# A two-layer model on one core: the phases after the recurrence as one program with one weight stream

## The chip, the cores and the metric

The kernel runs on one core of one Trainium2 chip. Its engines are named as the profile names them: PE is TensorE (matmul), PEld its weight loads, DVE is VectorE, ACT is ScalarE, POOL is GpSimd, SP is SyncE, which here only issues DMAs. The metric is device time in microseconds of one execution. Lower is better.

## The reference, cut to what matters

The input is one sequence of 512 tokens with 1024 channels (`x`). Two blocks follow each other, all in float32:

```python
h = rms_norm(x, a_norm);  x = x + rwkv7_time_mix(h, ...)        # recurrence, then y @ a_w_out   (2048 -> 1024)
h = rms_norm(x, b_norm);  c, b, u, g = split(h @ b_w_in, 4)     # 1024 -> 4 * 2048
y = b * conv3(c * u) * silu(g);  x = x + y @ b_w_out            # 2048 -> 1024
x = rms_norm(x, final_norm)                                     # end of the first model
h = rmsnorm(x, norm1_g);  proj = h @ w_in                       # 1024 -> 2560, start of the second
mixed = [rg_lru(...) * gelu(...), stick_breaking(...), diff_attention(...)]
x = x + mixed @ w_out                                           # 1024 -> 1024
h2 = rmsnorm(x, norm2_g);  gate, val = split(conv3(h2 @ w_ff_up) + b, 2)   # 1024 -> 2 * 2816
x = x + (silu(gate) * val) @ w_ff_down                          # 2816 -> 1024
return rmsnorm(x, final_g)
```

`rms_norm(x, g)` is `x * rsqrt(mean(x*x over channels) + 1e-6) * g`: for each token one number (the norm factor) times the channel's gain.

## The kernel before

Activations lie with channels on the 128 partitions and the 512 tokens along the row; a "chunk" is 128 channels of all tokens, so `x` has DC = 8 chunks, the inner width IC = 16, the feed-forward width FC = 22. Every large product is made of three float32r matmuls of 128x128 weights on 128x512 data, from numbers split in a high and a low part: high weights by high data, high weights by low data, low weights by high data (L141, L142, L143 in `products`). The high part of a tile is an ACT copy, the low part a DVE subtraction (`split_lo`, L148), for the weights and for the activations.

The program is a row of phases, each a block of its own with its own buffers and semaphores. At the end of a phase all engines meet in a barrier and its semaphores are cleared (`Sems.clear`), so that no engine, and no DMA, works on the next phase before all are done with this one. Up to 900 us run `lerp_phase` and `rwkv_phase` (norm, mixing, the recurrence), which end with the tensor `gate`, the recurrence's output. Behind them, in this order:

- `out1` (`project_phase`): splits `gate` in `y`, multiplies by `w_out1` and adds to `x`; 8 output chunks `n` of two weight units each, where a unit is 8 of the 128x128 tiles (512 KB) and 24 matmuls. It sums the squares of the new `x` (ACT square, DVE add, one matmul with `row_mean`, L1367).
- `conv` (`conv_phase`): `head_scalar`, `head_vector` and `head_tensor` first make the norm factor (ACT: `Ln`, then `Exp`, each with a table load), scale `x` by gain and factor on DVE, and split it in `h`; then 16 chunks of 4 units, with gates and a convolution of 3 taps on DVE and ACT.
- `out2`, then the norm between the models on `x` (`norm_vector`, L177) and the variance for the next norm.
- `in2` (`input_phase`): head as before, 20 units, of which 16 leave channels on partitions (`proj`) and 4 have the data as the stationary operand and leave tokens on partitions (`vals`); the gated linear recurrence (`lru`) is worked off beside them on ACT, DVE and POOL, and PE makes its gates (L1686).
- `mixer_phase`: both attentions, four heads one after the other.
- `out3`, `up` (`up_phase`, 22 chunks of 2 units, head as before), `down` (22 chunks deep, two units of 11 tiles for each output chunk), and the last norm with the store.

Weight loads are issued by SP into two raw buffers of a phase (four in `in2`) and wait until DVE has split what lay there. Most chunks of `conv`, `up` and the projections run in hardware loops (`Fori`). Where the buffers lie in a partition of SBUF is fixed by their sizes and their order. The program built from the kernel has them at these byte addresses:

```
                      start   start mod 64
h_hi, h_lo            43264, 59648     0    data of conv, in2, up
y_hi, y_lo            163808, 131040   32   data of out1, out2
m_hi, m_lo            212960, 196576   32   data of out3
ff_hi, ff_lo          184288, 139232   32   data of down
out1/conv/out2/up w   84224, 100608    0    weights, high and low
out3 w                96512, 104704    0
in2 w                 122144, 138528   32
down w                54528, 77056     0
```

## Time and profile before

| | |
|---|---|
| median of 3 runs | 2247.37 us (2241.43 to 2247.61) |
| profiled execution, its own time | 2243.56 us |
| its span, first to last instruction | 2241.8 us |
| share of the span with PE / DVE / ACT / POOL busy | 89% / 54% / 41% / 4% |
| mean granted TensorE clock | 0.946 |
| moved by DMA | 154.18 MB, mean 69 GB/s |

The span is read from the profiler's trace of one execution, 1.76 us shorter than that execution's own time. A busy PE means that some matmul is in flight: a 128x512 matmul is shown with about 0.39 us, while the next one starts 0.23 us after it, so starts, not durations, give the pace.

### The profile page before, as it was taken

How to read it: one execution, taken by the hardware profiler on the slowest of the kernel's cores; microseconds unless marked ns; L12 is line 12 of the kernel's file. 1: busy time of each engine (PE TensorE's matmuls, PEld its weight loads, DVE VectorE, ACT ScalarE, POOL GpSimd, SP SyncE). 2: the span in 40 equal slices, each digit the busy share in tenths (PEclk: the TensorE clock that was granted, in tenths of full speed). 3: DMA queues.
4: the chain of work that ended last, by engine and by line, in shares of the span. 5: the costliest groups of instructions: out<-in, count | busy, mean ns of one | idle time of the engine just before them, and what ended most of it. 6: DMA issues, size and time to landing. Idle time of an engine off the chain costs nothing. (4 is left out here: it accounts for less than half of the span.)

```text
span 2241.8 us, 45147 instructions
## 1 busy us (share of the span) xinstructions
PE 2004.5 (89%) x19062; PEld 1541.2 (69%) x19062; DVE 1204.2 (54%) x1913; ACT 918.2 (41%) x1412; POOL 95.3 (4%) x122
## 2 busy tenths in 40 slices
PE   5989799999999997889999998969966689999797
PEld 3678567676666665667888886857843368888686
DVE  5562367777777775425434443354346446666332
ACT  3342355554646454323323322245345435555321
POOL 2000000000000000000000000001112000000000
PEclk8999899999999998899999999989977789999899
DMA  3225211111111100413233232232000022222321
GB/s 113 73 83 148 89 38 40 29 43 37 38 41 38 42 18 2 150 56 113 94 94 102 85 94 81 69 113 93 1 0 1 24 89 94 94 94 94 103 81 60
DMA packets 49269, 154.18 MB, mean 69 GB/s; under 512 B 8272, under 2 KB 10576, under 8 KB 48592
## 3 DMA queue, kind: packets, MB, share of 16 engines
q1 hardware_dynamic: 48960, 149.65, 20.8%
q8 instruction: 132, 2.16, 0.4%
q10 hardware_dynamic: 144, 2.10, 0.3%
q14 instruction: 33, 0.27, 0.0%
HBM read 145.43 MB, written 6.29 MB: 68 GB/s over the span
## 5 line engine op out<-in xcount | busy, mean ns | idle before, releaser
L141 PE MATMUL bank<-h_hi,conv_whi 128*128 128x512 f32 x512 | 200.6, 392 | 9.0 <-DVE h_lo L148 9.0
L142 PE MATMUL bank<-h_lo,conv_whi 128*128 128x512 f32 x512 | 200.3, 391 | 0.0
L143 PE MATMUL bank<-h_hi,conv_wlo 128*128 128x512 f32 x512 | 200.2, 391 | 0.0
L141 PE MATMUL bank<-h_hi,up_whi 128*128 128x512 f32 x352 | 138.5, 393 | 9.9 <-DVE h_lo L148 9.0
L1424 DVE TENSOR_TENSOR x<-x,bank 128x512 f32<-128x512 f32 x32 | 22.0, 687 | 220.7 <-PE bank L143 220.7
L142 PE MATMUL bank<-h_lo,up_whi 128*128 128x512 f32 x352 | 138.1, 392 | 0.0
L143 PE MATMUL bank<-h_hi,up_wlo 128*128 128x512 f32 x352 | 138.0, 392 | 0.0
L141 PE MATMUL bank<-xg_hi,g_hi 128*128 128x512 f32 x256 | 104.1, 406 | 25.0 <-DVE xg_lo L148 16.9
L141 PE MATMUL bank<-y_hi,out_whi 128*128 128x512 f32 x256 | 103.1, 403 | 22.5 <-DVE y_lo L148 12.9
L141 PEld LDWEIGHTS bank<-h_hi,conv_whi 128*128 128x128 f32 x512 | 96.8, 189 | 29.8 <-DVE h_lo L148 9.8
L143 PEld LDWEIGHTS bank<-h_hi,conv_wlo 128*128 128x128 f32 x512 | 96.8, 189 | 20.3
L142 PEld LDWEIGHTS bank<-h_lo,conv_whi 128*128 128x128 f32 x512 | 96.8, 189 | 20.2
L763 ACT ACTIVATE swapT<-invT 64x256 f32<-64x256 f32 x160 | 66.4, 415 | 106.0 <-DVE invT L1221 57.4
L142 PE MATMUL bank<-y_lo,out_whi 128*128 128x512 f32 x256 | 102.7, 401 | 0.0
L143 PE MATMUL bank<-y_hi,out_wlo 128*128 128x512 f32 x256 | 102.5, 400 | 0.0
L142 PE MATMUL bank<-xg_lo,g_hi 128*128 128x512 f32 x256 | 101.8, 398 | 0.0
L143 PE MATMUL bank<-xg_hi,g_lo 128*128 128x512 f32 x256 | 101.8, 398 | 0.0
L1377 ACT ACTIVATE out_whi<-out_raw 128x1024 fp32r<-128x1024 f32 (+1 forms) x48 | 44.0, 917 | 134.2 <-DMA out_raw<-in_w_out 68.5
L1511 ACT ACTIVATE conv_whi<-conv_raw 128x1024 fp32r<-128x1024 f32 x64 | 67.6, 1056 | 58.1 <-PE bank L143 51.8
L1199 DVE TENSOR_TENSOR low<-bank,con 128x512 f32<-128x512 f32 x80 | 55.1, 689 | 60.2 <-PE bank L904 60.2
L148 DVE TENSOR_TENSOR g_lo<-g_raw,g_hi 128x1024 fp32r<-128x1024 f32 x32 | 40.8, 1276 | 86.5 <-ACT g_hi L383 86.5
L904 PEld LDWEIGHTS bank<-inv,LA 64*64 64x64 f32 x2560 | 47.0, 135 | 58.2 <-issue 58.0
(362 smaller groups left out, 4984.5 us busy)
## 6 DMA issues: line engine op xcount, KB each, us to landing
conv_raw<-in_w_conv SPq DMA_DIRECT2D x64, 512.0 KB, 3.5
up_raw<-in_w_up SPq DMA_DIRECT2D x44, 512.0 KB, 3.7
out_raw<-in_w_out SPq DMA_DIRECT2D x32, 512.0 KB, 4.0
down_raw<-in_w_down SPq DMA_DIRECT2D x16, 704.0 KB, 4.5
in_raw<-in_w_in SPq DMA_DIRECT2D x20, 512.0 KB, 3.6
g_raw<-in_w_g SPq DMA_DIRECT2D x16, 512.0 KB, 3.6
g_raw<-in_w_r SPq DMA_DIRECT2D x16, 512.0 KB, 4.0
w_k<-in_w_k SPq DMA_DIRECT2D x16, 512.0 KB, 3.5
```

Of the source, the lines that this page charges most:

```text
L141: pe.matmul(out, w_hi[:, w], x_hi[:, k, :], start=(first and n == 0), stop=False)
L142: pe.matmul(out, w_hi[:, w], x_lo[:, k, :], start=False, stop=False)
L143: m = pe.matmul(out, w_lo[:, w], x_hi[:, k, :], start=False, stop=(last and n == len(ks) - 1))
L148: return dve.tensor_tensor(lo, full, hi.bitcast(F32), ALU.subtract)
L763: act.activation(swapT[rows[1 - j], :, :], invT[rows[j], 1, :, :], ACT.Copy).then_inc(S("swap"), 1)
L904: m = pe.matmul(X[h][rows[j ^ h], cols(b)], LA[rows[j], h, b, 0, :], inv[rows[j], h, b, :], start=True, stop=True)
L1199: dve.tensor_tensor(low[:, :, :, :], heads(0), over2(C["level_mask"][:, lv * HD:(lv + 1) * HD]), ALU.mult).then_inc(S("low"), 1)
L1377: act.activation(w_hi[:, 2 * q + u, :], raw[:, u, :], ACT.Copy).then_inc(S("whi"), 1)
L1424: dve.tensor_tensor(x[:, n, :], x[:, n, :], bank[n % 2][:, :], ALU.add).then_inc(S("added"), 1)
L1511: act.activation(w_hi[:, j, :], raw[:, j % 2, :], ACT.Copy).then_inc(S("whi"), 1)
```

## The change

All phases behind the recurrence become one block, `dense_phase`, written out without loops.

- **One weight stream.** The 512 KB units of all seven products are one list (`UNITS`, 16 + 64 + 16 + 20 + 8 + 44 + 24 = 192 of them). SP loads them one after the other into two raw buffers, each as soon as DVE has split the unit two before it; ACT and DVE split unit g + 4 into a ring of four high and four low buffers once PE has used unit g (`split(g)`). `down` now takes three units (8, 8 and 6 tiles) for each output chunk.
- **No barrier between the products.** PE goes from one product to the next and waits by data: for the weights of its unit (`wlo`) and, in the first unit, for each chunk of its operand.
- **Norm factors behind the products.** In `out1`, `out2` and `out3` each new chunk of `x` is scaled by the gain alone and split at once (`h1_hi`, `h1_lo` and so on). The factor of each token is multiplied in where DVE takes the product out of PSUM: `u` and `sg` (and `cvr` for the third factor) in `conv`, `proj` and `vals` in `in2`, `z` in `up`. These reads of PSUM were ACT's in `conv` (`u`), `in2` and `up`, and are DVE's now. The sum of squares is finished with one matmul behind the first unit of the next product (`totals`). The norm of `x` between the models is done by DVE during the first units of `in2`.
- **Small work moved.** The constants of `lru` and attention are made during `out2`; `mixed` is split for `out3` partly in the second head of attention (`whole`, `part`).
- **Buffers over each other.** `h`, `y`, `m`, `ff` and the attention tensors share four regions. In the built program the weight ring begins at 51456 and 67840, `h` at 84224 and 100608, the high parts of `y`, `m` and `ff` at 116992 (all 0 mod 64), and their low parts in `gate` at 196576 (32 mod 64); the last six chunks of `ff_lo` are at 162048 (0 mod 64).

```diff
-            x = K["x"] = sbt(top, "x", [P, DC, T])
-            norms = top.enter_context(ExitStack())
-            h = K["h"] = pair(norms, "h", DC)
-            with ExitStack() as inner:
-                y = K["y"] = pair(inner, "y", IC, "right")
-                project_phase(K, "out1", y, IC, "w_out1", load_x=True, full=gate)
-                conv_phase(K)
-                project_phase(K, "out2", y, IC, "w_out2", norm="final_norm")
...
-                input_phase(K)
-                mixer_phase(K)
...
-            project_phase(K, "out3", y, DC, "w_out3", full=mixed)
...
-            up_phase(K)
-            norms.close()
-            project_phase(K, "down", ff, FC, "w_down", norm="final_g_2", squares=False, store=True)
+            dense_phase(K)
...
+def dense_phase(K):
...
+    RAW, RING = 2, 4
...
+    cut = lambda w, kt: [w[n, :, k * P:min(k + DC, kt) * P] for n in range(DC) for k in range(0, kt, DC)]
+    stage("out1", cut(ins["w_out1"], IC))
+    stage("conv", [ins["w_conv"][n, j] for n in range(IC) for j in range(4)])
+    stage("out2", cut(ins["w_out2"], IC))
+    stage("in2", [ins["w_in2"][k] for k in range(20)])
+    stage("out3", cut(ins["w_out3"], DC))
+    stage("up", [ins["w_up"][n, g] for n in range(FC) for g in range(2)])
+    stage("down", cut(ins["w_down"], FC))
+    LAST = len(UNITS)
...
+        raw = sbt(ctx, "raw", [P, RAW, DC * P])
+        w_hi, w_lo = (sbt(ctx, "w" + n, [P, RING, DC * P], F32R) for n in ("_hi", "_lo"))
...
+        zone, zone_at = place("zone", 2 * DC)
+        first, first_at = place("first", IC)
+        extra, extra_at = place("extra", 12)
+        gate_at = K["gate_at"]
...
+        h = [over("h_hi", zone_at, 0, DC), over("h_lo", zone_at, DC, DC)]
+
+        y = [over("y_hi", first_at, 0, IC), over("y_lo", gate_at, 0, IC)]
...
+            for g in range(LAST):
+                need(sp, S("wlo"), g - RAW + 1)
+                width = UNITS[g].shape[-1]
+                sp.dma_start(raw[:, g % RAW, 0:width], UNITS[g]).then_inc(S(f"w{g % RAW}"), 16)
...
+            def unit(g, to, src, ks, start, stop, ready=None):
+                pe.wait_ge(S("wlo"), g + 1)
+                for i, k in enumerate(ks):
+                    if ready:
+                        pe.wait_ge(S(ready), k + 1)
+                    hi, lo = src(k)
+                    whi, wlo = (w[:, g % RING, i * P:(i + 1) * P] for w in (w_hi, w_lo))
+                    begin, end = start and i == 0, stop and i == len(ks) - 1
+                    pe.matmul(to, whi, hi, start=begin, stop=False)
+                    pe.matmul(to, whi, lo, start=False, stop=False)
+                    last = pe.matmul(to, wlo, hi, start=False, stop=end)
+                last.then_inc(S("used"), 1)
+
+            def out_stage(tag):
+                at, src, kt, ready, _ = OUT[tag]
+                for n in range(DC):
+                    need(pe, S(tag + "_added"), n - 1)
+                    for u_ in range(per(tag)):
+                        unit(AT[tag] + per(tag) * n + u_, bank[at + n % 2][:, :], src,
+                             range(u_ * DC, min(u_ * DC + DC, kt)), u_ == 0, u_ == per(tag) - 1,
+                             ready if n == 0 else None)
+
+            def totals(tag):
+                for name, at in SUMS[tag]:
+                    pe.wait_ge(S(f"{tag}_sum_{name}"), DC - 1)
+                    pe.matmul(bank[at][:, :], C["row_mean"], sq[name][:, 0, :], start=True, stop=True)\
+                        .then_inc(S(f"{tag}_total_{name}"), 1)
...
+            def conv_stage():
+                for n in range(IC):
+                    for j in range(4):
+                        need(pe, S(("u", "cu", "sg", "full")[j]), n - 1)
+                        if n == 1 and j == 2:
+                            pe.wait_ge(S("out1_rstd"), 1)
+                        unit(AT["conv"] + 4 * n + j, bank[4 * ((n + 1) % 2) + j][:, :], of(h), range(DC), True, True,
+                             "h1_lo" if n == 0 else None)
+                        if n == 0 and j == 0:
+                            totals("out1")
...
+            def up_stage():
+                for n in range(FC):
+                    for g in range(2):
+                        need(pe, S("z"), 2 * (n - 2) + g + 1)
+                        unit(AT["up"] + 2 * n + g, bank[2 + 2 * (n % 2) + g][:, :], of(h), range(DC), True, True,
+                             "h3_lo" if n == g == 0 else None)
+                        if n == g == 0:
+                            totals("out3")
...
+            def split(g):
+                if g >= LAST:
+                    return
+                width = UNITS[g].shape[-1]
+                act.wait_ge(S(f"w{g % RAW}"), 16 * (g // RAW) + 16)
+                need(act, S("used"), g - RING + 1)
+                act.activation(w_hi[:, g % RING, 0:width], raw[:, g % RAW, 0:width], ACT.Copy).then_inc(S("whi"), 1)
...
+                    if gain:
+                        act.activation(h[0][:, n, :], x[:, n, :], ACT.Copy, scale=gains(gain, n))\
+                            .then_inc(S(f"h{step}_hi"), 1)
...
+            def out_stage(tag, step, extra_work=None):
+                at, _, _, _, gain = OUT[tag]
+                U = per(tag)
+                for n in range(DC):
+                    g = AT[tag] + U * n
+                    for u_ in range(U - 1):
+                        split(g + u_ + RING)
+                    dve.wait_ge(S("used"), g + U)
+                    if tag == "out1" and n == 0:
+                        dve.wait_ge(S("x"), 16)
+                    if tag == "out3":
+                        dve.wait_ge(S("x4"), n + 1)
+                    dve.tensor_tensor(x[:, n, :], x[:, n, :], bank[at + n % 2][:, :], ALU.add)\
+                        .then_inc(S(tag + "_added"), 1)
+                    split(g + U - 1 + RING)
+                    if gain:
+                        dve.wait_ge(S(f"h{step}_hi"), n + 1)
+                        dve.scalar_tensor_tensor(out=h[1][:, n, :], in0=x[:, n, :], scalar=gains(gain, n),
+                                                 in1=h[0][:, n, :].bitcast(F32), op0=ALU.mult, op1=ALU.subtract)\
+                            .then_inc(S(f"h{step}_lo"), 1)
+                    if n:
+                        for name, _ in SUMS[tag]:
+                            dve.wait_ge(S(f"{tag}_sq_{name}"), n + 1)
+                            dve.tensor_tensor(sq[name][:, 0, :], sq[name][:, 0, :], sq[name][:, 1, :], ALU.add)\
+                                .then_inc(S(f"{tag}_sum_{name}"), 1)
...
+                    if n == 0:
+                        split(g + RING)
+                        dve.wait_ge(S("out1_rvar"), 1)
+                    dve.wait_ge(S("used"), g + 1)
+                    need(dve, S("cu"), n)
+                    dve.tensor_tensor(u, bank[b][:, :], rs[:, 1, :], ALU.mult).then_inc(S("u"), 1)
+                    if n:
+                        split(g + RING)
+                    dve.wait_ge(S("used"), g + 2)
+                    dve.wait_ge(S("u"), n + 1)
+                    need(dve, S("taps1"), n)
+                    need(dve, S("tap2"), n)
+                    dve.tensor_tensor(cu, bank[b + 1][:, :], u, ALU.mult).then_inc(S("cu"), 1)
+                    split(g + 1 + RING)
...
+                    dve.tensor_tensor(sg, bank[b + 2][:, :], rs[:, 0, :], ALU.mult).then_inc(S("sg"), 1)
+                    split(g + 2 + RING)
+                    dve.wait_ge(S("taps1"), n + 1)
+                    dve.scalar_tensor_tensor(out=cv, in0=cv, scalar=0.5, in1=rs[:, 0, :], op0=ALU.mult,
+                                             op1=ALU.mult).then_inc(S("cvr"), 1)
...
+            def in_stage():
+                for k in range(20):
+                    g = AT["in2"] + k
+                    if k == 0:
+                        split(g + RING)
+                        dve.wait_ge(S("out2_rvar"), 1)
+                        dve.wait_ge(S("out2_total_next"), 1)
+                        dve.tensor_tensor(bank[7][:, :], bank[7][:, :], rs[:, 1, :], ALU.mult)\
+                            .then_inc(S("next_var"), 1)
+                        dve.wait_ge(S("out2_rstd"), 1)
+                        for j in range(DC):
+                            dve.scalar_tensor_tensor(out=x[:, j, :], in0=x[:, j, :], scalar=V["final_norm"][:, j:j + 1],
+                                                     in1=rs[:, 0, :], op0=ALU.mult, op1=ALU.mult).then_inc(S("x4"), 1)
+                            if j == 3:
+                                dve.wait_ge(S("out2_rstd2"), 1)
+                                dve.tensor_tensor(rs[:, 1, :], rs[:, 1, :], rs[:, 0, :], ALU.mult).then_inc(S("rr"), 1)
+                        dve.wait_ge(S("rr"), 1)
...
+                    if k < 16:
+                        dve.tensor_tensor(proj[:, k, :], bank[k % 4][:, :], rs[:, 1, :], ALU.mult)\
+                            .then_inc(S("copied"), 1)
...
+                    if n == 1:
+                        for k in range(4):
+                            part(k)
...
+                for n in range(FC):
+                    g = AT["up"] + 2 * n
+                    for q in range(2):
+                        at = FC * q + n
+                        tap = lambda k: V["conv_ff_w_2"][:, 2 * FC * k + at:2 * FC * k + at + 1]
+                        if n == q == 0:
+                            split(g + RING)
+                            dve.wait_ge(S("out3_rstd"), 1)
+                        dve.wait_ge(S("used"), g + q + 1)
+                        need(dve, S("u0"), 2 * (n - 1) + q + 1)
+                        need(dve, S("tap1"), 2 * (n - 1) + q + 1)
+                        dve.tensor_tensor(z[:, q, :], bank[2 + 2 * (n % 2) + q][:, :], rs[:, 0, :], ALU.mult)\
+                            .then_inc(S("z"), 1)
+                        if n or q:
+                            split(g + q + RING)
...
```

On PE, at the end of `out1` and the start of `conv` (`y` is the operand of `out1`, `h` that of `conv`; before:)

```order
L141 MATMUL bank<-y_hi,out_whi 128x512
L142 MATMUL bank<-y_lo,out_whi 128x512
L143 MATMUL bank<-y_hi,out_wlo 128x512
L1328 REGISTER_ALU
L1328 COMPARE_AND_BRANCH
L1367 MATMUL bank<-out_sq_next,con 128x512 [waits out1_sum_next]
L1313 UNCONDITIONAL_BRANCH
L1492 UNCONDITIONAL_BRANCH [waits barrier_Pool_Activation_PE_DVE_SP_release]
L141 MATMUL bank<-h_hi,conv_whi 128x512 [waits conv_wlo,conv_norm_lo]
L142 MATMUL bank<-h_lo,conv_whi 128x512
```

and now (`extra` holds the squares; the rows left out are the other chunks of the first unit):

```order
L1367 MATMUL bank<-y_hi,w_hi 128x512
L1368 MATMUL bank<-y_lo,w_hi 128x512
L1369 MATMUL bank<-y_hi,w_lo 128x512
L1367 MATMUL bank<-h_hi,w_hi 128x512 [waits dense_h1_lo,dense_wlo]
L1368 MATMUL bank<-h_lo,w_hi 128x512
...
L1367 MATMUL bank<-h_hi,w_hi 128x512 [waits dense_h1_lo]
L1368 MATMUL bank<-h_lo,w_hi 128x512
L1369 MATMUL bank<-h_hi,w_lo 128x512
L1384 MATMUL bank<-extra,con 128x512 [waits dense_out1_sum_plain]
L1367 MATMUL bank<-h_hi,w_hi 128x512 [waits dense_h1_lo,dense_wlo]
```

The sum of squares and the barrier stood between the two products; now the sum stands one unit later and the barrier is gone.

On DVE, one chunk of `up` in its loop before (`up_wlo` is the low part of the weights; the ISA and register rows cost no busy time):

```order
L2175 SCALAR_TENSOR_TENSOR up_u<-up_z,up_col,up_u 128x511
L2179 SCALAR_TENSOR_TENSOR up_u<-up_z,up_col,up_u 128x510
L2183 SCALAR_TENSOR_TENSOR up_u<-up_th,up_u 128x512
L2187 SCALAR_TENSOR_TENSOR up_full<-up_u 128x512
L2158 ISA
L148 TENSOR_TENSOR up_wlo<-up_raw,up_whi 128x1024
L2158 REGISTER_ALU
L148 TENSOR_TENSOR up_wlo<-up_raw,up_whi 128x1024
L148 ISA
L148 TENSOR_TENSOR ff_lo<-up_full,ff_hi 128x512
```

and now (`tmp` holds `z`, `u` and the product, `rs` the norm factor, `par` the taps):

```order
L2022 TENSOR_TENSOR tmp<-bank,rs 128x512
L148 TENSOR_TENSOR w_lo<-raw,w_hi 128x1024
L2027 SCALAR_TENSOR_TENSOR tmp<-tmp,par 128x511
L2030 SCALAR_TENSOR_TENSOR tmp<-tmp,par 128x510
L2034 SCALAR_TENSOR_TENSOR tmp<-tmp 128x512
L2022 TENSOR_TENSOR tmp<-bank,rs 128x512
L148 TENSOR_TENSOR w_lo<-raw,w_hi 128x1024
L2027 SCALAR_TENSOR_TENSOR tmp<-tmp,par 128x511
L2030 SCALAR_TENSOR_TENSOR tmp<-tmp,par 128x510
L2039 SCALAR_TENSOR_TENSOR tmp<-tmp 128x512
L148 TENSOR_TENSOR ff_lo<-tmp,ff_hi 128x512
```

Two reads of PSUM have come to DVE's queue, and each weight split stands behind one of them.

## Rows read from the trace of the kernel before

**Rows 1.** The page, part 1: busy time, share and instructions of each engine.

```profile
PE 2004.5 (89%) x19062; PEld 1541.2 (69%) x19062; DVE 1204.2 (54%) x1913; ACT 918.2 (41%) x1412; POOL 95.3 (4%) x122
```

**Rows 2.** Busy time by stretch: start:end, us, engines (instructions), clock, DMA share, GB/s.

```profile
907.40:999.20 91.80, 91.75 (x384) 73.65 (x384) 34.66 (x43) 25.92 (x35) 0.00 (x0) 0.98 0.28 99
999.20:1011.60 12.40, 1.21 (x4) 0.34 (x3) 6.06 (x11) 7.55 (x9) 0.00 (x0) 0.69 0.28 91
1011.60:1362.70 351.10, 351.10 (x1536) 290.26 (x1536) 156.92 (x201) 104.43 (x131) 0.00 (x0) 0.99 0.30 93
1362.70:1372.40 9.70, 0.14 (x2) 0.03 (x1) 2.67 (x4) 2.74 (x3) 0.00 (x0) 0.66 0.35 109
1372.40:1463.80 91.40, 91.40 (x384) 73.25 (x384) 29.39 (x34) 22.91 (x28) 0.00 (x0) 0.98 0.24 81
1463.80:1485.50 21.70, 2.06 (x6) 0.70 (x5) 12.32 (x18) 13.62 (x16) 0.95 (x1) 0.68 0.28 104
1485.50:1632.40 146.90, 141.66 (x784) 118.95 (x784) 67.12 (x90) 64.08 (x91) 17.18 (x12) 0.99 0.20 64
1632.40:1641.20 8.80, 0.04 (x1) 0.00 (x0) 3.30 (x4) 4.94 (x6) 0.00 (x0) 0.67 0.00 0
1641.20:1785.60 144.40, 101.26 (x284) 53.58 (x285) 78.94 (x246) 74.98 (x170) 27.13 (x21) 0.70 0.01 4
1785.60:1832.10 46.50, 46.48 (x192) 37.18 (x192) 22.08 (x35) 16.04 (x28) 0.00 (x0) 0.96 0.24 80
1832.10:1844.50 12.40, 1.22 (x4) 0.31 (x3) 6.44 (x16) 7.46 (x9) 0.00 (x0) 0.69 0.28 90
1844.50:2087.90 243.40, 242.53 (x1056) 200.12 (x1056) 162.58 (x226) 122.28 (x176) 0.00 (x0) 0.99 0.28 90
2087.90:2102.20 14.30, 0.20 (x2) 0.03 (x1) 5.14 (x7) 5.17 (x6) 0.00 (x0) 0.67 0.29 101
2102.20:2227.60 125.40, 125.35 (x528) 100.57 (x528) 31.80 (x29) 23.10 (x21) 0.00 (x0) 0.98 0.25 81
2227.60:2241.80 14.20, 1.13 (x2) 0.30 (x2) 6.75 (x10) 4.51 (x5) 0.00 (x0) 0.68 0.38 148
```

**Rows 3.** The same view of stretches inside stages: conv's start, out1, conv, in2.

```profile
1011.60:1017.60 6.00, 6.00 (x14) 4.74 (x15) 5.22 (x7) 3.75 (x5) 0.00 (x0) 0.50 0.57 179
...
920.00:990.00 70.00, 70.00 (x302) 56.41 (x301) 22.15 (x25) 16.46 (x19) 0.00 (x0) 1.00 0.27 90
1050.00:1350.00 300.00, 300.00 (x1326) 248.42 (x1325) 130.07 (x165) 87.79 (x109) 0.00 (x0) 1.00 0.30 95
...
1552.00:1572.00 20.00, 20.00 (x88) 16.09 (x86) 9.16 (x10) 11.24 (x15) 3.08 (x3) 1.00 0.17 54
```

**Rows 4.** The page, part 6: issues, KB each, median us from issue to landing.

```profile
conv_raw<-in_w_conv SPq DMA_DIRECT2D x64, 512.0 KB, 3.5
```

**Rows 5.** Timeline of DVE and ACT (start, us): out1's end, conv, up.

```profile
999.28 0.69 DVE L1424 TENSOR_TENSOR x<-x,bank 128x512 f32<-128x512 f32 x1 [9.12 <-PE bank L143]
...
1101.73 1.07 ACT L1511 ACTIVATE conv_whi<-conv_raw 128x1024 fp32r<-128x1024 f32 x1 [3.63 <-PE bank L143]
...
1102.83 1.23 DVE L148 TENSOR_TENSOR conv_wlo<-conv_raw,conv_whi 128x1024 fp32r<-128x1024 f32 x1 [0.41 <-ACT conv_whi L1511]
...
1933.59 0.75 DVE L2175 SCALAR_TENSOR_TENSOR up_u<-up_z,up_col,up_u 128x511 f32<-128x511 f32 x1 [1.48 <-ACT up_u L2137]
...
1936.29 0.77 ACT L2137 ACTIVATE up_u<-bank,up_col 128x512 f32<-128x512 f32 x1
```

**Rows 6.** Timeline: the norm between the models on DVE; one table load on ACT.

```profile
1470.50 5.39 DVE L177 SCALAR_TENSOR_TENSOR x<-x,par,out_rstd 128x512 f32<-128x512 f32 x8 [3.93 <-ACT out_rstd L1407]
...
1477.17 1.28 ACT L169 ACT_TABLE_LOAD   x1 [6.71 <-PEq L131]
```

**Rows 7.** Timeline: PE's gates of lru in in2.

```profile
1548.01 1.98 PE L1686 MATMUL bank<-lru_xc,wbd 128*128 128x512 f32 x4 [2.32 <-DVE lru_xc L1804]
```

**Rows 8.** Timeline: last Exp of in2 on ACT; first scores of attention on DVE.

```profile
1636.85 0.63 ACT L1737 ACTIVATE lru_g<-lru_g 128x512 f32<-128x512 f32 x1
...
1646.70 0.49 DVE L2000 SCALAR_TENSOR_TENSOR pr<-bank,bias 128x128 f32<-128x128 f32 x2 [0.19 <-PE bank L1906]
```

1361 lines of the change are left out of this document (574 added, 787 removed).

## Prediction

> **What bounds the kernel now.** I read the page first: PE is busy in 89% of the span, DVE in 54%, ACT in 41% [rows 1]. PE is the bound, so the questions are how fast its matmuls follow each other and where it stands. The second view is the table by stretch from the end of the recurrence on [rows 2]. It falls into products (PE busy throughout) and joins (PE busy for 0.04 to 2.1 us): 12.4, 9.7, 21.7, 8.8, 12.4 and 14.3 us, and the last 9.0 us of the attention stretch, in which PE starts nothing until `out3` (my reading of the 144.4 us row; its busy time also holds attention's own small waits). Together 88.3 us without matmuls of a product. The third view is the same table inside stages [rows 3]. Its counts include the two matmuls cut by the edges, so `out1` has (302 - 2) in 70 us, one every 0.2333 us, and `conv` (1326 - 2) in 300 us, one every 0.2266 us. At `conv`'s start the granted clock is half (1.2 of 2.4 GHz) for 6.0 us with 14 matmuls, 0.427 us each; every other product after a join starts so too, which its clock of 0.96 to 0.99 in [rows 2] shows.
>
> **Two paces.** `in2` shares its data tile `h` with `conv` and `up`, yet has 88 - 2 matmuls in 20 us, 0.2333 us [rows 3]. What sets it apart is its weight buffers, which begin 32 bytes past a multiple of 64; `out1`, `out2`, `out3` and `down` have aligned weights and their data at such an address; `conv` and `up` have both aligned. From the whole stretches: `up` 243.4 us / 1056 and `down` 125.4 / 528 give 0.2305 and 0.2375, in which the slow starts are contained. I take it that an operand off 64 bytes costs its matmul 0.0067 us. In the changed program weights, `h` and the high parts are aligned and only low parts in `gate` are not, so one matmul in three pays: 0.2266 + 0.0067 / 3 = 0.2289 us.
>
> The Trainium skill (TensorE: Matmul & The Clock Gate, "Wait — 56ns, not 53.3ns?") gives one start-to-start time for 512 columns at full clock, 215.7 ns, whatever the buffers. No stretch here is that fast. By one pace for each product, unchanged by addresses, this term is nothing and the sum comes out 9.4 us higher.
>
> **The change, stretch by stretch** (before in [rows 2]; after worked out):
>
> - `out1`, 91.8: starts behind the recurrence's barrier as now, 10 matmuls at half clock, 4.3; then 374 x 0.2289 = 85.6. Together 89.9, a gain of 1.9.
> - Join to `conv`, 12.4. The last chunk of `x` is added in 0.69 us on DVE [rows 5], while ACT splits a weight unit (1.07), then copies `h1_hi` (0.8, as L2137). DVE behind its own split (1.23) makes `h1_lo` (0.75). From the last start of `out1`: 0.4 until the add begins, so about 3.6 us. PE has seven other chunks in the first unit, 7 x 3 x 0.227 = 4.8 us. Covered with 1.2 us to spare. What stays is the sum of squares, 1.1 us as in the tail (1.13 busy there) [rows 2], behind the first unit; its square and add are done 4.3 us after the end, PE comes at 5.4. Gain 11.3.
> - `conv`, 351.1: 1536 x 0.2266 = 348.1. Gain 3.0. A chunk lasts 21.8 us; DVE has 4 splits (4.9) and 10 operations of 0.69 to 0.75 (7.2), 12.1 in all, ACT 6.
> - Join to `out2`, 9.7: `out2`'s first units are in the ring; the last `y2_lo` comes some 3 us after `conv`'s end and is wanted by the sixteenth chunk, 10.3 us on. Gain 9.7.
> - `out2`, 91.4: 384 x 0.2289 = 87.9. Gain 3.5. The constants of `lru` come here, twenty operations of 128x4; DVE has some 6 of each chunk's 11 us to do.
> - Join to `in2`, 21.7: as the first join, with two sums, 2.2. Gain 19.5. What takes its place is the norm factor, which the first unit's product now needs on DVE: first total at 6, four table loads of 1.28 [rows 6] and four functions on ACT, x's norm 5.4 on DVE [rows 6], so `proj` 0 is copied some 20 us into `in2`. PE wants that bank at unit 4, 4 x 5.44 + 2.2 = 24.0. Covered by 4 us.
> - `in2`, 146.9: the 384 matmuls of 512 columns lose 0.0067 each (2.6), the half clock at the start goes (7 matmuls, 1.4), the factor's four transposing matmuls cost 0.5. PE's waits for `lru` stay: [rows 7] shows 2.3 us before a gate, because DVE and ACT still carry the previous part; that queue gets one more PSUM read and loses nothing. Gain 3.5.
> - Join and attention, 8.8 + 144.4, to 1785.6. `in2`'s last Exp ends at 1637.5; the first scores stand at 1646.7 [rows 8]. Without the barrier, ACT takes |z| right behind that Exp, DVE ends `lru` (0.69, 1.22, 0.69) and takes the four relus (1.6) in about 4.8 us: scores at 1642.3. Gain 4.4. At the end, `out3` has its first four chunks split already, in the second head, behind waits for PE there. It starts as attention's last matmul ends, 9.0 us earlier, and meets the others in time. Gain 13.4 with both.
> - `out3`, 46.5: half clock for 14 matmuls (6.0), then 178 x 0.2289: 46.8. Loss 0.3.
> - Join to `up`, 12.4: as the first. Gain 11.3.
> - `up`, 243.4: 1056 x 0.2266 = 239.3. Gain 4.1.
> - Join to `down`, 14.3: the last `ff_lo` is wanted by the 22nd chunk, 14.4 us on, and comes at about 6. Gain 14.3.
> - `down`, 125.4: 528 x 0.2266 plus 128 misaligned x 0.0067 = 120.5. Gain 4.9.
> - Tail, 14.2: the same chain.
>
> Sum 1.9 + 11.3 + 3.0 + 9.7 + 3.5 + 19.5 + 3.5 + 13.4 - 0.3 + 11.3 + 4.1 + 14.3 + 4.9 = 100.1. Span 2241.8 - 100.1 = 2141.7; that execution's own time is 1.8 above its span, and the median of the runs 3.8 above that: 2147 us.
>
> **Edits costed at nothing.** The tightest cover is DVE in `up`. Between two `ff_lo` stand two PSUM reads (0.69), two splits (1.15 apart), four taps of 0.75, three products and the split of 0.69, with two waits for ACT (tanh 0.6, `ff_hi` 0.6): 10.3 us against PE's 10.9. If the cover is gone, each 0.1 us over 10.9 costs 2.2 us. Behind a waiting DVE stand the weight splits, and for them wait PE and, two units on, SP's next load. Loads: 512 KB land in 3.5 us [rows 4] and are split in 2.3, under 5.4 a unit; SP's six small loads before `in2` are moved into `out1`, ahead of unit 17, which is wanted 27 us later. Bounds of what no row shows: a low operand off alignment costs nothing (-3) or all three matmuls of its tile (+6); PE's waits in `in2` go (-5) or double (+5); attention gains nothing from its earlier start (+4); each join leaves up to 2 us (+10).
>
> **The rivals.**
>
> - *The joins close only in part.* The ring is not full when a product ends, and PE waits for data. For it: only two raw buffers, and DVE splits a unit only after its PSUM work. Against it: a unit's round (3.5 + 1.1 + 1.2) is under two units of PE. A load issued at the join would cost its landing and splits, 5.8, and half clock behind it, 2.8, at five joins: +43, 2190 us; half of that is as likely. 15%.
> - *Loops written out run slower.* `conv`, `up` and the projections leave their loops; if fetching instructions set 0.2333 us, 2592 matmuls pay 0.0067: 17 us, 2164 us. Against it: `out1` is a loop too and has that pace. By the Trainium skill (Runtime: NRT & Kernel Launch, "Instruction fetch mechanics") code in sequence is fetched ahead and a taken branch is what stalls; by that this rival costs nothing. No row here times a fetch. 6%.
> - *The change gains little.* DVE falls behind in `in2`, where the bank of unit 0 is free at 20 and wanted at 24, and in attention, so that the two largest gains (19.5 and 13.4) go: 2180 us. 4%.
> - *Slower than before.* DVE in `up` becomes the bound and PE waits in each of 22 chunks, each wait followed by matmuls at half clock. It decides from a cycle of 10.9 + (100 + 7) / 22 = 15.8 us on: 2254 us and more. Against it: the chain above is 10.3 us, from durations in rows. 3%.
>
> The likeliest case, all joins closed and the paces as worked out, has 72%, and 2134 to 2166 of its own.
>
> **How the numbers follow.** I give the likeliest case's 2147. The low end takes -3, -5 and a few more of attention; the high end reaches half of the first rival and the loops' 17. 0.3% (7 us) is about what a measurement of this kernel can tell from no change. Faster: all but the last rival and a sliver of larger mishaps, 95%; same 2%; slower 3%.
>
> **What would show it.** PE starting `h_hi` matmuls within 0.3 us of the last `y_hi`, at full clock; 0.227 us between starts in `in2` and `conv`, about 0.229 in `out1` and `down`; the clock at 1.0 from `out1` to the end of `in2`, low only in attention. The forecast is wrong if PE waits for `w_lo`, for `z` or for `tmp`, or if starts in `conv` stand 0.233 us apart.

## The result and the profile after

The changed kernel takes 2150.82 us in the median of 4 runs (2144.45 to 2152.77), the kernel before 2244.58 in 4 (2241.43 to 2247.61). The ratio is 0.9578, 95% interval 0.955 to 0.9605: 94 us faster, where 100 were forecast (2147; 2134 to 2166 for the likeliest case).

The page, part 1, against [rows 1]:

```profile
PE 1988.2 (92%) x19070; PEld 1535.4 (71%) x19070; DVE 1268.7 (59%) x1955; ACT 884.5 (41%) x1333; POOL 99.5 (5%) x122
```

The table by stretch, cut at the first matmul of each product, against [rows 2] (columns as there). In order: `out1`, `conv`, `out2`, `in2`, attention, `out3`, `up`, `down`, tail:

```profile
909.60:1001.30 91.70, 91.63 (x384) 73.69 (x385) 43.71 (x53) 33.24 (x45) 0.00 (x0) 0.98 0.41 137
1001.30:1350.40 349.10, 349.10 (x1539) 288.67 (x1538) 185.85 (x225) 99.47 (x118) 0.00 (x0) 1.00 0.29 97
1350.40:1439.10 88.70, 88.70 (x385) 72.17 (x384) 40.80 (x64) 32.88 (x44) 0.00 (x0) 1.00 0.30 96
1439.10:1587.00 147.90, 142.13 (x797) 120.34 (x796) 80.32 (x95) 61.65 (x76) 24.89 (x13) 0.99 0.22 72
1587.00:1727.20 140.20, 98.42 (x283) 52.38 (x284) 84.79 (x250) 76.30 (x173) 23.60 (x19) 0.71 0.01 4
1727.20:1774.10 46.90, 45.47 (x194) 36.16 (x193) 24.81 (x32) 20.77 (x29) 0.00 (x0) 1.00 0.24 79
1774.10:2014.40 240.30, 240.30 (x1059) 198.58 (x1058) 187.41 (x240) 111.14 (x136) 0.00 (x0) 1.00 0.29 96
2014.40:2136.00 121.60, 121.55 (x529) 99.01 (x527) 35.90 (x40) 25.85 (x30) 0.00 (x0) 1.00 0.26 75
2136.00:2150.90 14.90, 1.12 (x2) 0.30 (x2) 6.76 (x10) 4.51 (x5) 0.00 (x0) 0.62 0.36 141
```

No stretch between the products is a join any more: PE is busy for all of `conv`, `out2`, `up` and `down`, at a granted clock of 1.00, where each product began at half clock before. PE's timeline at the first join (start, us) shows how `conv` follows `out1`:

```profile
1001.10 0.39 PE L1369 MATMUL bank<-y_hi,w_lo 128*128 128x512 f32 x1
1001.33 0.40 PE L1367 MATMUL bank<-h_hi,w_hi 128*128 128x512 f32 x1
1001.57 0.39 PE L1368 MATMUL bank<-h_lo,w_hi 128*128 128x512 f32 x1
```

0.23 us from the last matmul of one to the first of the other, where 12.7 lay. What happens beside it on DVE and ACT is the chain that the prediction laid out:

```profile
1001.53 0.69 DVE L1745 TENSOR_TENSOR x<-x,bank 128x512 f32<-128x512 f32 x1 [3.22 <-PE bank L1369]
...
1002.56 0.71 ACT L1533 ACTIVATE h_hi<-x,par 128x512 fp32r<-128x512 f32 x1
...
1003.83 0.75 DVE L1750 SCALAR_TENSOR_TENSOR h_lo<-x,par,h_hi 128x512 fp32r<-128x512 f32 x1
```

The last `h_lo` is there at 1004.6, 3.5 us behind the last start of `out1` (3.6 forecast); the first unit comes to that chunk 5.0 us behind it, and PE does not wait.

Against the forecast, from first start to first start (us; the forecasts are the prediction's terms, with each sum of squares counted where it now stands, behind the first unit of the next product: 1.1 in `conv` and `up`, 2.2 in `in2`):

| stretch | before | after | gained | forecast |
|---|---|---|---|---|
| up to `out1` | 907.5 | 909.7 | -2.2 | 0 |
| `out1` and join | 104.1 | 91.7 | 12.4 | 14.3 |
| `conv` and join | 360.8 | 349.1 | 11.7 | 11.6 |
| `out2` and join | 113.1 | 88.7 | 24.4 | 25.2 |
| `in2` to the first scores | 161.2 | 157.0 | 4.2 | 5.7 |
| scores to `out3` | 138.9 | 131.0 | 7.9 | 9.0 |
| `out3` and join | 58.9 | 46.9 | 12.0 | 12.1 |
| `up` and join | 257.7 | 240.3 | 17.4 | 17.3 |
| `down` and tail | 139.6 | 136.5 | 3.1 | 4.9 |
| sum (span) | 2241.8 | 2150.9 | 90.9 | 100.1 |

Three things are off. The part ahead of the change came 2.2 us late in this execution; it begins `out1` anywhere from 904.6 to 911.1 us in the profiles below, though its code is the same, which is about as wide as the scatter between runs. `in2` gave 1.5 less, attention 1.1. And the products with low parts in `gate` (`out1`, `out2`, `out3`, `down`) are slower than 0.2289 a matmul. `conv`, `out3` and `up` came out within 0.1.

The time is nearer to the forecast than its terms are, and that is luck. The span missed by 9.2 us (2150.9, forecast 2141.7), the median by 3.8. The forecast had added 3.8 us because the profiled execution of the kernel before was that much under its median; here the profiled execution is 1.9 us over it.

### The profile page after: what moved, and what is told of

Same layout as the page of the kernel before. It is cut to its first block, busy times and chain, and to the rows that moved or that the text cites. A ratio compares the mean times of both kernels' runs of the same rounds, so it can differ in the third digit from the quotient of the medians.

```text
span 2150.9 us, 43896 instructions
## 1 busy us (share of the span) xinstructions
PE 1988.2 (92%) x19070; PEld 1535.4 (71%) x19070; DVE 1268.7 (59%) x1955; ACT 884.5 (41%) x1333; POOL 99.5 (5%) x122
## 4 chain that ended last, share of the span: by engine, by line
PE 52%; DVE 4%; ACT 1%; issue 0%; DMA 0%; ACTq 0%; DVEq 0%
PE bank L1368 15%; PE bank L1367 15%; PE bank L1369 15%; PE bank L1482 1%; PE bank L1428 1%; PE bank L1427 1%; PE bank L1426 1%; PE bank L1462 1%; DVE tmp L1862 0%; PE bank L1489 0%; PE bank L1456 0%; DVE tmp L1997 0%; PE bank L1465 0%; PE bank L1411 0%; DVE tmp L1942 0%; DVE zone L1971 0%
## 5 line engine op out<-in xcount | busy, mean ns | idle before, releaser
L1524 ACT ACTIVATE w_hi<-raw 128x1024 fp32r<-128x1024 f32 (+1 forms) x192 | 201.7, 1051 | 573.9 <-PE bank L1369 521.5
L1367 PE MATMUL bank<-h_hi,w_hi 128*128 128x512 f32 x992 | 389.4, 393 | 0.0
L1368 PE MATMUL bank<-h_lo,w_hi 128*128 128x512 f32 x992 | 386.4, 390 | 0.0
L1369 PE MATMUL bank<-h_hi,w_lo 128*128 128x512 f32 x992 | 386.3, 389 | 0.0
L148 DVE TENSOR_TENSOR w_lo<-raw,w_hi 128x1024 fp32r<-128x1024 f32 (+1 forms) x192 | 232.9, 1214 | 167.6 <-ACT w_hi L1524 167.5
L1367 PEld LDWEIGHTS bank<-h_hi,w_hi 128*128 128x128 f32 x992 | 186.6, 188 | 40.4 <-issue 1.6
L1368 PEld LDWEIGHTS bank<-h_lo,w_hi 128*128 128x128 f32 x992 | 186.5, 188 | 40.3 <-issue 1.7
L1369 PEld LDWEIGHTS bank<-h_hi,w_lo 128*128 128x128 f32 x992 | 186.5, 188 | 38.7
L141 PE MATMUL bank<-xg_hi,g_hi 128*128 128x512 f32 x256 | 104.9, 410 | 25.2 <-DVE xg_lo L148 17.1
L1367 PE MATMUL bank<-y_hi,w_hi 128*128 128x512 f32 x256 | 101.8, 398 | 12.8 <-DVE y_lo L148 12.8
L1368 PE MATMUL bank<-y_lo,w_hi 128*128 128x512 f32 x256 | 102.3, 400 | 0.0
L148 DVE TENSOR_TENSOR g_lo<-g_raw,g_hi 128x1024 fp32r<-128x1024 f32 x32 | 40.8, 1277 | 90.9 <-ACT g_hi L290 90.9
```

Of the source, the lines that this page charges most:

```text
L141: pe.matmul(out, w_hi[:, w], x_hi[:, k, :], start=(first and n == 0), stop=False)
L148: return dve.tensor_tensor(lo, full, hi.bitcast(F32), ALU.subtract)
L1367: pe.matmul(to, whi, hi, start=begin, stop=False)
L1368: pe.matmul(to, whi, lo, start=False, stop=False)
L1369: last = pe.matmul(to, wlo, hi, start=False, stop=end)
L1524: act.activation(w_hi[:, g % RING, 0:width], raw[:, g % RAW, 0:width], ACT.Copy).then_inc(S("whi"), 1)
```

## Experiments: what sets the matmul's pace

The forecast had an operand off a 64-byte multiple cost its matmul 0.0067 us. After the change, inside `out1` and `out2`:

```profile
920.00:990.00 70.00, 70.00 (x302) 56.32 (x301) 28.91 (x32) 20.61 (x25) 0.00 (x0) 1.00 0.40 127
1360.00:1430.00 70.00, 70.00 (x305) 56.94 (x304) 33.32 (x56) 28.05 (x39) 0.00 (x0) 1.00 0.30 97
```

That is 0.2333 and 0.2310 us (less two cut matmuls each; the starts in the trace are 0.2333 and 0.2311 apart in the mean), though only one matmul in three has an operand off 64. So `out1` gained nothing by its addresses. Two kernels move buffers by 32 unused bytes, and nothing else. **after_aligned**:

```diff
+            sbt(top, "pad", [P, 8], side="right")
             gate = K["gate"] = sbt(right, "gate", [P, IC, T], side="right")
```

> The changed kernel with 32 unused bytes above gate, so that the low parts of y, m and ff begin at a multiple of 64. Theory (address): all products have 0.2267 us between starts, against 0.2333 in out1 and out3, 0.2311 in out2 and 0.2298 over down in the changed kernel's trace. That is 384 x 0.0067 + 192 x 0.0067 + 384 x 0.0044 + 528 x 0.0031 = 2.6 + 1.3 + 1.7 + 1.6 = 7.2 us less than 2150.8: about 2144. Rival (the pace belongs to the product, its banks or its data, not to the address): same spacings, 2151.

2146.1 us (5 runs, ratio 0.9567, 0.9554 to 0.958). That is 4.7 us less than the changed kernel, where the theory had 7. All four products came to 0.2289 from start to start (307 matmuls in 70 us), neither 0.2267 nor unchanged.

**before_aligned**: the same line in the kernel before, and `sbt(ctx, "in2_pad", [P, 8])` below the weights of `in2`.

> The kernel before with 32 unused bytes above gate and 32 below the weight buffers of in2, so that every large operand begins at a multiple of 64. Theory (address): out1, out2, in2, out3 and down go from 0.2333 to 0.2267 us between starts, (3 x 384 + 192 + 528) x 0.0067 = 12.5 us less than 2244.6: about 2232; in2 may keep part of its 2.6, as its waits for lru take it back. Rival (loops or the product set the pace): 0.2333 as before, 2245.

2243.23 against 2243.44 us (ratio 0.9999, 0.999 to 1.0008), with 302 matmuls in 70 us of `out1` as before. The theory as it stood, with a step at 64 bytes, fell. Its operands lay at 64 past a multiple of 128 now, and those of `conv` and `up`, which always had 0.2267, lie at multiples of 256. So the next pads were 96 bytes (`[P, 24]`) and 224 (`[P, 56]`), **after_pad96** and **after_pad224**:

> The changed kernel with 96 unused bytes above gate: the low parts begin at a multiple of 128 that is not one of 256. In the two kernels with 32 bytes operands went to 64 past a multiple of 128: the kernel before kept 0.2333 us, and in the changed one, whose high parts are at a multiple of 256, out1, out2, out3 and down all came to 0.2289 = 0.2267 + 0.0067 / 3. New theory: an operand that is 64 past a multiple of 128 still costs its own matmul 0.0067 us, one at 32 more than that. If 128 is enough, all products come to 0.2267 and this run ends at about 2143; if 256 is wanted, they stay at 0.2289 and it ends at 2146. Rival (the distance between the buffers counts, not the start): no pattern by the start, 0.2289 or more.

> The same with 224 unused bytes, so that the low parts begin at a multiple of 256, as all other large operands of the changed kernel do. Theory (start address): 0.2267 us in every product, 2143. Rival (the distance between the buffers counts, or each product has its own pace): 0.2289 or more somewhere, 2146.

And **before_pad224**, both pads at 224 bytes:

> The kernel before with 224 unused bytes above gate and 224 below the weights of in2: every operand of the large products begins at a multiple of 256. Theory (start address): out1, out2, in2, out3 and down go from 0.2333 to 0.2267 us between starts, 1872 matmuls x 0.0067 = 12.5 us less, 2231; in2's 2.6 of it may go back into its waits. Rival (the products' loops set 0.2333, as 32 bytes changed nothing there): 2243.

PE inside `out1`, the same 70 us in five kernels; first 32 bytes in the changed kernel (after_aligned):

```profile
920.00:990.00 70.00, 70.00 (x307) 57.43 (x307) 30.12 (x34) 22.80 (x28) 0.00 (x0) 1.00 0.40 127
```

96 bytes (after_pad96):

```profile
920.00:990.00 70.00, 70.00 (x304) 56.91 (x303) 30.04 (x34) 22.90 (x28) 0.00 (x0) 1.00 0.39 124
```

224 bytes (after_pad224):

```profile
920.00:990.00 70.00, 70.00 (x311) 57.95 (x310) 30.13 (x34) 22.80 (x28) 0.00 (x0) 1.00 0.41 129
```

The kernel before with 32 bytes, then with 224:

```profile
920.00:990.00 70.00, 70.00 (x302) 56.10 (x301) 22.19 (x25) 16.47 (x19) 0.00 (x0) 1.00 0.26 89
```

```profile
920.00:990.00 70.00, 70.00 (x310) 57.97 (x309) 22.33 (x25) 16.48 (x19) 0.00 (x0) 1.00 0.26 89
```

The counts give the pace to some 0.001 us; the mean distance of the starts in the trace is more exact:

| low parts begin at (mod 256) | `out1` | `out2`, `down` to chunk 15 |
|---|---|---|
| 224 (changed kernel) | 0.2333 | 0.2311 |
| 192 (after_aligned) | 0.2289 | 0.2289 |
| 128 (after_pad96) | 0.2311 | 0.2289 |
| 0 (after_pad224) | 0.2267 | 0.2267 |

The means are 0.2267 plus none, one, two or three thirds of 0.0067.

This does not mean that one, two or three matmuls of each tile pay, as the single starts show:

- In `out2` of after_pad96, behind the low matmul the next start is 0.2342 us on, behind the two others 0.2267 and 0.2258: the low one alone pays.
- In `out2` of after_aligned, with the same mean, all three have 0.2283 to 0.2293.
- In `out1` of after_pad96 the chunks alternate between 0.2295 and 0.2328.
- In `down` of after_aligned chunks 16 to 18, whose operands all begin at multiples of 256, still have 0.2330, 0.2302 and 0.2305 in each of the eight rounds, and only chunks 19 to 21 have 0.2267. So a matmul behind others with a bad operand can pay too.

With all operands of a product at multiples of 256 it has 0.2267 in either kernel; with data at 224 or 192, or weights at 32 or 64 (`in2` of the two kernels before), it is 0.2333. That start addresses set the pace is shown, by moving buffers alone, and that 64 or 128 is not enough. One other rule fits as well and was not tried: that the distance between data and weights within 256 bytes counts, not their starts. In every slow product here the two differ, and no kernel moves both by the same. Why the same low part costs more in `out1` than in `out2` stays open. after_pad224 took 2140.78 us (4 runs, 0.954, 0.9525 to 0.9556), 10.0 less than the changed kernel: in its trace the four products give 7.2 of it, as the theory had, and `in2` 1.6 (see below). after_pad96 took 2144.32 (0.956, 0.9544 to 0.9576); before_pad224 took 2237.09 against 2244.71 (0.9969, 0.9957 to 0.9981), 7.6 us of the 12.5 expected. The trace shows where the rest went: from first to last start `out1` lost 2.5, `out3` 1.3 and `down` 3.4, all as expected; `out2` only 1.2, since it began with 14 matmuls at half clock where there had been 8; and `in2` up to its last unit of channels nothing (102.3 us, 102.0 before): its faster matmuls met longer waits for `lru` (6.1 us, 5.2 before) and half clock behind one of them, which leads to the next question.

## Experiments: who sets the pace of in2

DVE's timeline in the changed kernel, from the end of unit 11 to the gates of `lru` (in the bracket: idle before, and what ended it), and those gates on PE:

```profile
1514.77 1.23 DVE L148 TENSOR_TENSOR w_lo<-raw,w_hi 128x1024 fp32r<-128x1024 f32 x1 [0.46 <-ACT w_hi L1524]
1517.24 0.69 DVE L1883 TENSOR_TENSOR tmp<-tmp,extra 128x512 f32<-128x512 f32 x1 [1.24 <-ACT tmp L1609]
1519.18 0.69 DVE L1886 SCALAR_TENSOR_TENSOR tmp<-tmp 128x512 f32<-128x512 f32 x1 [1.25 <-ACT tmp L1611]
1519.90 1.22 DVE L1890 TENSOR_TENSOR_SCAN tmp<-tmp 128x512 f32<-128x512 f32 x1
1521.23 0.69 DVE L1893 SCALAR_TENSOR_TENSOR gate<-tmp,extra 128x512 f32<-128x512 f32 x1
1521.84 0.69 DVE L1915 TENSOR_TENSOR first<-bank,rs 128x512 f32<-128x512 f32 x1
1522.44 1.22 DVE L148 TENSOR_TENSOR w_lo<-raw,w_hi 128x1024 fp32r<-128x1024 f32 x1
1523.57 3.56 DVE L1862 SCALAR_TENSOR_TENSOR tmp<-first,par,tmp 128x511 f32<-128x511 f32 x3
...
1527.18 2.56 PE L1411 MATMUL bank<-tmp,extra 128*128 128x512 f32 x4 [2.73 <-DVE tmp L1862]
```

The chain begins with the end of a unit, for the weight split of ACT and DVE waits for `used`, and `lru`'s last part stands behind that split. From there (1513.5) it takes 13.7 us, over two table loads, scan, PSUM read, split and three taps. PE has two units in that time. The faster those are, the longer PE waits: 10.9 us of work where there were 11.2, and 2.7 us of idle where [rows 7] has 2.3, in this execution with seven matmuls at half clock behind it. The gates stand 26.51 us apart (1500.67, 1527.18), the same two before the change 26.69 (1548.01, 1574.70): of the 0.64 us that four faster units save, PE keeps 0.18. **after_lru_first** takes `lru`'s last part ahead of the split, on ACT and DVE alike:

```diff
                 for k in range(20):
+                    if k >= 4 and k % 4 == 3:
+                        lru(k // 4 - 1, 3)
                     split(AT["in2"] + k + RING)
...
-                    if k >= 4:
+                    if k >= 4 and k % 4 < 3:
                         lru(k // 4 - 1, k % 4)
```

> The changed kernel, in2 alone changed: in every fourth unit ACT and DVE do the last part of lru ahead of the split of the next weights and ahead of the wait for that unit, instead of behind them. Theory (the gates' waits are the chain from a unit's end over split, Ln, Exp, scan, mixed, PSUM read, split and taps): PE's waits of 0.9, 2.2 and 3.1 us before the gates shrink to under 0.5 each and the half clock behind the last goes (about 6 us), and the scores of the first head come some 5 us earlier, since lru's last part no longer waits for the last unit of vals: 2140. Rival 1 (the gates wait for the taps themselves behind the PSUM read and split of the same unit): only the 5 us at the start of attention, 2146. Rival 2 (later weight splits starve PE): 2151 or more.

2140.4 us (5 runs, 0.9537, 0.9524 to 0.955), 10.4 less than without it: the first theory. Of the 12.1 us between the two traces, 8.3 lie between `in2`'s start and the first scores and 1.4 in an earlier start of `out1`. The gates come 25.0 us apart (the second at 1496.94 with 0.3 us of idle, the third at 1521.96 with 1.3, not under 0.5), and the clock stays at 1.00:

```profile
1436.90:1534.60 97.70, 95.64 (x409) 75.70 (x408) 62.34 (x74) 49.74 (x61) 15.52 (x9) 1.00 0.26 86
```

against 102.3 us for the same units without the edit. The first scores stand 148.7 us behind `in2`'s start, not 157.0. One DVE subtraction of this stretch, usually 0.69 us, took 2.19 while POOL worked, from 1574.57 to 1576.76 beside POOL's `TENSOR_SCALAR` that ended at 1576.66.

The half clock itself is priced by after_pad224, where `in2` has the same addresses and the same three waits (5.0 us in both). From `in2`'s start to its last unit of channels, and from just before the last gate on; first the changed kernel, then after_pad224:

```profile
1439.10:1541.40 102.30, 97.29 (x409) 76.64 (x409) 62.71 (x74) 48.35 (x59) 16.09 (x9) 0.98 0.26 82
1525.80:1533.00 7.20, 5.82 (x15) 3.77 (x16) 4.27 (x6) 1.89 (x3) 0.00 (x0) 0.76 0.31 103
```

```profile
1432.60:1533.30 100.70, 95.68 (x409) 75.71 (x409) 62.70 (x74) 48.38 (x59) 16.11 (x9) 1.00 0.25 84
1519.30:1526.50 7.20, 5.83 (x22) 4.16 (x23) 4.26 (x6) 1.90 (x3) 0.00 (x0) 1.00 0.28 95
```

The spell costs 1.6 us.

**after_best** (both edits, 32 bytes) and **after_best2** (both, 224 bytes):

> Both edits together, aligned low parts and lru's last part first. If the two theories hold they don't touch the same stretch, and their gains add up: 7 and 11 us, 2133. If the pace is a property of the product: the time of the kernel with lru's last part first.

> The changed kernel with low parts at a multiple of 256 and lru's last part ahead of split and wait in in2. By the start address it is some 2 to 3 us under the 2135.1 of the version with 32 bytes: 2132.5. By the rival the same 2135.

2135.13 us (5 runs, 0.9516, 0.9503 to 0.9529) and 2135.88 (5 runs, 0.9515, 0.9502 to 0.9528). The gains of the two single edits, 4.7 and 10.4, add up in the first (15.7). The second is not faster than the first within the noise: its products do take some 3 us less in the trace, but the work between `in2`'s channels and `out3` takes 1.7 more, and its `out1` began at 909.2 us, that of the first at 906.7. Both beat the changed kernel by about 15 us.

## Experiments: what the joins were worth

**after_cut** takes the stream's head start away at four joins:

```diff
+        edges = [AT[t] for t in ("conv", "out2", "in2", "down")]
         @block.sync
         def _(sp):
             for g in range(LAST):
+                if g in edges:
+                    sp.wait_ge(S("used"), g)
                 need(sp, S("wlo"), g - RAW + 1)
```

> The changed kernel with the weight stream cut at four joins: SP issues the first load of conv, out2, in2 and down only when PE has used the last unit of the product before (out3 and up keep the stream). All data waits and the norm factors stay. Theory: what the stream gives at a join is the landing of a load (3.5), its two splits (2.3) and the half clock behind the pause (2.8), 8.6 us each: 4 x 8.6 = 34 more, 2185. Rival (loads at a join are hidden by the first unit's wait for h or y anyway): under 4 us each, 2166 or less.

**after_norm_first** keeps the stream and lets PE wait for the norm factor (`totals`, and ACT's `factor`, moved ahead of the first unit and of the split; in `in2` and `up` likewise):

```diff
                     for j in range(4):
...
+                        if n == 0 and j == 0:
+                            totals("out1")
+                            pe.wait_ge(S("out1_rstd"), 1)
                         unit(AT["conv"] + 4 * n + j, ...)
-                        if n == 0 and j == 0:
-                            totals("out1")
```

> The changed kernel with PE waiting for the norm factor ahead of the first unit of conv, in2 and up, as the kernel before had to; the stream stays. Theory, from the rows of the tail and of the table loads: the last sum is ready 4.3 us behind the last matmul, its matmul and the wait behind it 0.8, then a table load and Ln (2.0) and a table load and Exp (2.0, 2.7 with two of them): 9 us at up, 10 at conv, some 15 at in2 (a second Ln and Exp and half of x's norm), with 2.8, 2.8 and 1.5 of half clock, less the 1 us the sum costs now: 11 + 12 + 16 = 39 more, 2190. Rival (the join's price is the barrier and the cold ring, and the norm chain runs beside it): under 15 in all, 2166.

**after_both_joins** is both:

> Both of them. At conv and in2 the load and the norm chain start at the same moment, so the longer one, the norm's, covers the load; out2 and down pay the load alone: 39 + 2 x 8.6 = 56 more than 2151, 2207. If the two parts added up independently it would be 73 more, 2224. What is then still missing to the 2244.6 of before is addresses, the small work and attention.

| kernel | us (4 runs) | more than 2150.8 | expected |
|---|---|---|---|
| after_cut | 2192.35 (ratio 0.977, 0.9754 to 0.9786) | 41.5 | 34 |
| after_norm_first | 2180.28 (0.9728, 0.9702 to 0.9754) | 29.5 | 39 |
| after_both_joins | 2228.47 (0.9936, 0.9918 to 0.9955) | 77.7 | 56 |

(The kernel before ran at 2243.16 us beside these three and at 2244.58 beside the changed kernel, so the differences are good to some 2 us.) The stream alone is worth more than expected, and the reason is a queue. ACT and DVE in after_cut at `conv`'s start:

```profile
1011.75 1.06 ACT L1528 ACTIVATE w_hi<-raw 128x1024 fp32r<-128x1024 f32 x1 [5.16 <-DMA raw<-in_w_conv]
...
1018.35 0.71 ACT L1537 ACTIVATE h_hi<-x,par 128x512 fp32r<-128x512 f32 x1
...
1012.85 1.23 DVE L148 TENSOR_TENSOR w_lo<-raw,w_hi 128x1024 fp32r<-128x1024 f32 x1 [4.40 <-ACT w_hi L1528]
...
1019.62 0.75 DVE L1754 SCALAR_TENSOR_TENSOR h_lo<-x,par,h_hi 128x512 fp32r<-128x512 f32 x1
```

The copies that make the last `h` stand behind splits of weights that are still in flight, so PE stops twice: 6.1 us for the first unit, then 5.1 in its last chunk:

```profile
1020.42 0.80 PE L1371 MATMUL bank<-h_hi,w_hi 128*128 128x512 f32 x1 [4.67 <-DVE h_lo L1754]
```

With both, the sum of squares stands behind the same splits: its matmul comes 19.4 us after `out1`'s last start, not 4.1 as in after_norm_first. The two parts don't hide each other, as I expected; they queue up (77.7 against 71 for the sum of the two). after_norm_first cost less than expected. PE paused 9.6, 13.3 and 8.9 us where I had 10, 15 and 9, for the first table load ran while ACT waited for the sum; that is 2.2 us. `in2` had no half clock behind its last gate this time (1.6), and `conv` began with 7 matmuls at half clock, where 2.8 us, some 14 matmuls, were reckoned (1.4). The rest is not worked out.

**after_up_dve2** tests the cover that the prediction called the tightest:

```diff
                     split_lo(dve, ff[1](n), ufull, ff[0](n)).then_inc(S("ff_lo"), 1)
+                    for e in range(2):
+                        need(dve, S("more"), 2 * n + e)
+                        dve.tensor_tensor(rs[:, 1, :], x[:, 0, :], x[:, 1, :], ALU.add).then_inc(S("more"), 1)
```

> The changed kernel with two more additions of 0.69 us (128x512, SBUF, result unused) on DVE behind each of the 22 ff_lo of up. Theory (the prediction's chain: 10.3 us of waits and work against PE's 10.9 a chunk): 10.3 + 1.4 = 11.7 us a chunk, 0.8 over PE's: 22 x 0.8 = 17 us more, 2168. Rival (busy time decides: DVE is busy for 184 of 234 us of up, 2.3 us idle a chunk): nothing, 2151.

2149.94 us (4 runs, 0.9592, 0.9572 to 0.9612), the same as without within the scatter. But not for the rival's reason. DVE's timeline, one chunk apart, shows a cycle of 11.26 us, over PE's 10.9:

```profile
1901.89 1.41 DVE L2045 TENSOR_TENSOR rs<-x 128x512 f32<-128x512 f32 x2
...
1913.15 1.41 DVE L2045 TENSOR_TENSOR rs<-x 128x512 f32<-128x512 f32 x2
```

and PE did not wait in `up` at all: 240.3 us from first to first start. DVE fell behind by 0.4 us a chunk, some 8 us over 22, and PE has credit for that: PSUM banks of two chunks and weights four units ahead. The debt shows once, in `down`, where PE waited for the last low part:

```profile
2025.75 0.50 PE L1367 MATMUL bank<-ff_hi_end,w_hi 128*128 128x512 f32 x1 [2.13 <-DVE ff_lo_end L148]
```

`down` and tail take 139.0 us, 136.5 without the additions: this is all that came of the 8. Without the additions the cycle would be 9.9 us (11.26 less 1.41, an estimate), so the chain of 10.3 in the prediction was 0.4 too long, and the step "each 0.1 us over 10.9 costs 2.2 us" was wrong: most of an overrun is paid from the credit.

## Why the prediction was right

- **The joins** (79.5 us of the 100.1, both ends of attention included). Right in place, size and mechanism: the rows of `conv`, `out3` and `up` are within 0.1 us, those of `out1` and `out2` miss what their pace explains. after_both_joins loses 77.7 us by the two waits alone. That this is near 79.5 is chance: attention's 13.4 is not in it, so 66.1 is what it should be held against, and its waits queue up as they did not in the kernel before (24.8 us of pause at `conv`, 12.7 there). It shows that the two waits can cost what the joins did. What the barrier costs beside them was not run.
- **The first rival (ring not full)** did not happen: behind a join no product but `out3` waits in its first unit, and that for `m_lo`, not for weights. The price put on it, 8.6 us a join, was too low: 10.4 in after_cut.
- **Paces.** The step that failed is "an operand off 64 bytes costs its matmul 0.0067 us". Two paces by address are right, and `in2` did go from 0.2333 to 0.2267; but 64 is not the step (256 is enough, 64 and 128 are not), and the price does not stay with the matmul that has the bad operand: behind the high, low and last matmul of a tile the next start is 0.2344, 0.2348 and 0.2308 us on in `out1`, and 0.2280, 0.2333 and 0.2321 in `out2`, where the prediction had 0.2267, 0.2333 and 0.2267. The term was mis-sized by 1.7 us in `out1` (384 x 0.0044), 0.8 in `out2`, some 0.8 in `out3` and in `down`. The reading of one pace for each product, whatever the addresses, is ruled out by after_pad224.
- **in2.** The term was mis-sized by 1.5 us: it had no half clock behind a gate's wait. "PE's waits for `lru` stay" is right for their sum (5.2 us before, 5.0 after), but not for each: the second shrank by 0.5, where the factor's four matmuls now stand ahead of it, and the third grew from 2.3 to 2.7, since read and split, with its wait by `used`, lie on the chain that sets the gates. Behind that third wait came the spell at half clock. Its terms give 100.7 us to the last unit of channels; the changed kernel took 102.1, and after_pad224, without the spell, 100.5. That the wait by `used` makes the chain late is shown by after_lru_first; that the added read alone would, was not tried. The sign of being wrong "if PE waits for `tmp`" did come, by these waits; it contradicts the prediction's own term, which keeps them.
- **Attention.** First scores 5.0 us behind the start of `lru`'s last Exp (1591.17, 1596.21), where it was 9.9, and `out3` starts as attention ends. 1.1 us were lost; the second head, into which the four copies and splits have moved, lasts 34.2 us against 33.2 from its first matmul to the next head's.
- **out3** came out at 46.9 as forecast (46.8), by errors that cancel: no half clock, as attention's last matmuls run right into it (clock 1.00), but 0.2333 a matmul and a wait of 1.4 us for the last `m_lo`.
- **down and tail** gained 3.1, not 4.9: 0.8 is the pace, 0.7 a slower tail (15.4 us behind the last start, 14.6 before). "The same chain" holds up to the last store, issued 11.8 us behind the last start in both. Behind it POOL clears the phase's semaphores, in two instructions of 0.20 and 0.65 us, where the last phase before had 0.05 and 0.09. That the whole block's semaphores are cleared at once there is the likely reason; no run tries it.
- **Loops written out** cost nothing: 0.2267 us in all of `conv` and `up`. The Trainium skill (Runtime: NRT & Kernel Launch, "Instruction fetch mechanics") has code in sequence fetched ahead; the trace agrees. The Trainium skill's 215.7 ns for 512 columns (TensorE: Matmul & The Clock Gate, "Wait — 56ns, not 53.3ns?") is reached nowhere: the best pace of any product here is 226.7 ns.

## What to carry to other kernels

Between two products that keep the bound engine busy, price the pause, the cold clock behind it and whatever in-order queue mixes weight splits with results; taking the barrier away pays in full only if the stream is ahead (after_cut gives 41.5 of the 94 us back), as the two parts of the join queue behind each other when it isn't. Before pricing a faster engine, look for the chain that it waits for: a wait that starts at the engine's own progress (`used`) takes back what the engine gains, and moving one step ahead of that wait gave 10 us. An overloaded helper engine costs little until the buffers' credit is spent (2.5 us for an overrun of 8), so compare its excess times the number of rounds with that credit, not with zero.
